# One rounding step of seven weight blocks per layer moved from GpSimd to ScalarE, in a two-layer hybrid backbone

## The reference

```python
def _token_mixers(h, pl, lambda_init, rope, ctx_kv):
    z = h @ pl['w_in']                  # 1024 -> 2816 columns: hyena 768, conformer 512, q, k, v 512 each
    ...
    if ctx_kv is None:
        k_all, v_all = k, v             # prompt: no rotation
    else:
        q = _apply_axial_rope(q, rope)  # sample: x*cos + partner(x)*sin
        k = _apply_axial_rope(k, rope)
        k_all = jnp.concatenate([ctx_kv[0].astype(dt), k], axis=1)
        v_all = jnp.concatenate([ctx_kv[1].astype(dt), v], axis=1)
    y_at = _diff_attention(q, k_all, v_all, lam, lambda_init, pl['subln_g'])
```

## Time and profile before

| | |
|---|---|
| time, median of 3 runs | 4292.77 us (4286.78 to 4298.58) |
| profiled execution, its own time | 4303.47 us |
| its span in the trace | 4301.5 us |
| mean granted TensorE clock | 0.943 of full |
| PE busy | 3737.7 us (87%) |
| DVE busy | 2407.0 us (56%) |
| POOL busy | 1510.2 us (35%) |
| ACT busy | 1052.5 us (24%) |

### The profile page before, as it was taken

The page is one execution under the profiler, slowest core; times in us unless marked ns, Lnnn a source line. Parts: engine busy times, 40 slices in busy tenths (PEclk is TensorE's granted clock), DMA queues, the critical chain, the costliest instruction groups (busy, mean ns, idle before and its releaser), DMA issues. The chain is left out here.

```text
span 4301.5 us, 51163 instructions
## 1 busy us (share of the span) xinstructions
PE 3737.7 (87%) x19550; PEld 3174.2 (74%) x19550; DVE 2407.0 (56%) x2998; ACT 1052.5 (24%) x1932; POOL 1510.2 (35%) x735
## 2 busy tenths in 40 slices
PE   7969989788759999999939998978794999999992
PEld 5768867577648888888828886767673888888881
DVE  2323554777575555555580365577667555555567
ACT  1011121367232111111141111147614111111115
POOL 0032656510242333323263275750033333223324
PEclk9999999899879999999968998989997999999996
DMA  5456654541301111111006664544220111111101
GB/s 155 129 185 194 184 167 121 169 112 59 113 20 30 40 40 35 37 38 40 20 16 204 198 178 155 160 137 100 77 89 10 40 40 37 33 40 40 40 11 49
DMA packets 360972, 380.86 MB, mean 89 GB/s; under 512 B 17951, under 2 KB 301709, under 8 KB 359470
## 3 DMA queue, kind: packets, MB, share of 16 engines
q1 hardware_dynamic: 247074, 233.40, 18.8%
q10 hardware_dynamic: 113676, 144.23, 10.4%
HBM read 286.34 MB, written 82.84 MB: 86 GB/s over the span
## 5 line engine op out<-in xcount | busy, mean ns | idle before, releaser
L638 POOL TENSOR_TENSOR RH<-RAW,ONE 128x1024 fp32r<-128x1024 f32 x256 | 504.1, 1969 | 2084.3 <-PE PS L730 863.8
L730 PE MATMUL PS<-HH,RH 128*128 128x512 f32 (+1 forms) x2784 | 615.1, 364 | 224.8 <-DVE HL L1683 63.8
L730 PEld LDWEIGHTS PS<-HH,RH 128*128 128x128 f32 x2784 | 479.3, 194 | 310.2 <-issue 154.7
L730 PE MATMUL PS<-HL,RH 128*128 128x512 f32 (+1 forms) x2784 | 701.7, 372 | 0.0
L640 POOL TENSOR_TENSOR RL<-RAW,RH 128x1024 fp32r<-128x1024 f32 x256 | 637.0, 2488 | 20.1
L730 PE MATMUL PS<-HH,RL 128*128 128x512 f32 (+1 forms) x2784 | 599.8, 358 | 0.0
L1919 DVE TENSOR_TENSOR SB<-RB 128x512 f32<-128x512 f32 (+1 forms) x192 | 205.5, 1070 | 644.0 <-ACT RB L1557 644.0
L1935 DVE SCALAR_TENSOR_TENSOR XT<-PS,ADA,XT 128x512 f32<-128x512 f32 (+1 forms) x768 | 474.2, 655 | 134.5 <-PE PS L1108 132.6
L730 PEld LDWEIGHTS PS<-HL,RH 128*128 128x128 f32 x2784 | 477.6, 193 | 57.3
L730 PEld LDWEIGHTS PS<-HH,RL 128*128 128x128 f32 x2784 | 466.3, 190 | 69.8
L1557 ACT ACTIVATE RB<-PS 128x512 f32<-128x512 f32 (+1 forms) x192 | 101.2, 527 | 1481.4 <-PE PS L730 1480.2
(11 more groups left out here) (224 smaller groups left out, 5370.9 us busy)
## 6 DMA issues: line engine op xcount, KB each, us to landing
RAW<-in_w_mlp_dram SPq DMA_DIRECT2D x128, 512.0 KB, 4.0
RAW<-const_dram SPq DMA_DIRECT2D x68, 512.0 KB, 3.9
ADW<-in_w_ada_dram ACTq DMA_DIRECT2D x60, 512.0 KB, 4.3
RAW<-in_w_in_dram SPq DMA_DIRECT2D x44, 512.0 KB, 4.7
ADW<-in_w_ada_dram SPq DMA_DIRECT2D x36, 512.0 KB, 3.7
x_scratch<-XT SPq DMA_DIRECT2D x4, 2560.0 KB, 13.8
z_scratch<-ZST ACTq DMA_DIRECT2D x40, 256.0 KB, 2.3
QH<-q_hi SPq DMA_DIRECT2D x32, 320.0 KB, 9.5
```

Source lines behind the costliest of these rows:

```text
L638: nc.gpsimd.tensor_tensor(RH[:, s, :], RAW[:, p, :], ONE[:].broadcast_to([128, 1024]), ALU.mult).then_inc(hi_split.sem, 1)
L730: mm = pe.matmul(out, w[:, s, k * 128:(k + 1) * 128], m(k), start=(n == 0 and k == 0), stop=(n == 2 and k == KT - 1))
```

## The change

For the seven blocks 17 to 23 of each layer (keys' last tile, the four value blocks, the first two forward-DFT blocks) the high part is made by ScalarE with an ACTIVATE Copy instead of by GpSimd; GpSimd waits for it on a new semaphore and makes the low part as before. ScalarE does this at the end of tiles 11 to 17, between the eight partner DMAs and `store_high`. GpSimd's own semaphore now counts 121 splits per layer. An unused semaphore is removed.

```diff
+FIRST_HI, SCALAR_HI = 17, 7
...
-        hi_split = signal("hi_split", BLOCKS)
+        hi_split = signal("hi_split", BLOCKS - SCALAR_HI)
+        hi_scalar = signal("hi_scalar", SCALAR_HI)
...
-        inv_done = signal("inv_done", 0)
...
                 pool.wait_ge(blk_used.sem, blk_used.at(l, b - RING + 1) + i * per_i)
-                nc.gpsimd.tensor_tensor(RH[:, s, :], RAW[:, p, :], ONE[:].broadcast_to([128, 1024]), ALU.mult).then_inc(hi_split.sem, 1)
-                pool.wait_ge(hi_split.sem, hi_split.at(l, b + 1) + i * per_i)
+                if FIRST_HI <= b < FIRST_HI + SCALAR_HI:
+                    pool.wait_ge(hi_scalar.sem, hi_scalar.at(l, b + 1 - FIRST_HI))
+                else:
+                    nc.gpsimd.tensor_tensor(RH[:, s, :], RAW[:, p, :], ONE[:].broadcast_to([128, 1024]), ALU.mult)\
+                      .then_inc(hi_split.sem, 1)
+                    own = b if b < FIRST_HI else b - SCALAR_HI
+                    pool.wait_ge(hi_split.sem, hi_split.at(l, own + 1) + i * per_i)
                 nc.gpsimd.tensor_tensor(RL[:, s, :], RAW[:, p, :], RH[:, s, :].bitcast(F32), ALU.subtract)\
...
+                def high_of_block(b):
+                    s, p = slot(l, b), b % 2
+                    act.wait_ge(raw_in[p].sem, raw_in[p].at(l, 16 * (b // 2 + 1)))
+                    act.wait_ge(blk_used.sem, blk_used.at(l, b - RING + 1))
+                    S.activation(RH[:, s, :], RAW[:, p, :], ACT.Copy).then_inc(hi_scalar.sem, 1)
...
                     if i >= 0:
                         partners(i)
+                    if 0 <= n + RING - FIRST_HI < SCALAR_HI:
+                        high_of_block(n + RING)
                     if i > 0:
                         store_high(i - 1)
```

## The result

The changed kernel takes 4327.86 us (median of 7 runs, 4315.74 to 4339.25) against 4292.14 us before (7 runs): ratio 1.0084, interval 1.0063 to 1.0105, that is 27 to 45 us slower. Forecast were 4330 us and slower.

A forecast was written before the change was run, and what follows sets the result against it. From tile 11 on, a ring of ACT and POOL, not PE, was taken to set the pace. Turns of 36.8 us plus 2 x 0.5 for the clock made 37.8; on 4292.77 that is 4330.6, predicted 4330, range 4311 to 4349.

The forecast's parts named there:

- The ring: ACT and POOL wait on each other per tile: high part, evacuation, DMA issue, landing, rotation; about 17.8 us a turn.
- the row of 579.51: Layer 0's last key transpose, behind the first value tile; its wait was read as ending 3.48 us before 579.51.
- Removed work: POOL's RH instruction, 14 times, 27.9 us, lying ahead of waits for partner DMAs; gain: nothing.
- The price of a turn: Eighth issue to next rotation 6.51 us, formerly the landing; five turns per layer, 17.5 and 17.1 us more.
- One sign of being right: POOL's RL of blocks 17 to 22 idles 5 to 7 us ahead of it, released by ACT's RH.
- The turn from tile 14 to 15: ACT itself is last there, with conformer store, load and sigmoid; the Copy costs its own length, 1.1 us.
- S: Stage from ScalarE's evacuation of tile 11's chunk 2 to the key transpose behind the first value tile; 110.2, 110.7 us before.
- PE's waits: ADW some 2 to 3 us around tile 15, then 6 to 8 us ahead of each key transpose; not added.
- The third rival: PE at 1.2 GHz for longer stretches, key tiles too; up to 28 us, half taken, 4345; chance 0.13.
- The clock's term: Slower PE clock around each layer's last wait; between 0 and 3.5 us per layer, 0.5 taken.

The follow-up runs named there:

- evac_first: The kernel before, with ScalarE evacuating chunk 2 ahead of the rotated head's high part instead of behind it: 4279.72 us, ratio 0.9956.
- copy_ahead: The changed kernel with ScalarE's Copy ahead of the eight partner DMAs instead of behind them: 4303.37 us, ratio 1.0012.
- both_mended: The changed kernel with chunk 2 evacuated first and the Copy ahead of the partner DMAs: 4280.85 us, ratio 0.9962.
- three_blocks: The changed kernel with only blocks 17, 18 and 19 getting their high part from ScalarE: 4315.43 us, ratio 1.0045.
- wait_only: The kernel before plus a 64-column ScalarE Copy of constants, awaited by GpSimd ahead of the low part of blocks 17 to 23: 4319.56 us, ratio 1.0046.

## Why the prediction was right

1. **The ring bounds the stage.** Right: evac_first takes PE's evacuation out of it and the waits of 15.0 us go. Two readings on the way were off. In the query tiles of layer 0 the ring did not set the pace: its turns there (17.09, 17.28 and 17.15 us between evacuations) were shorter than PE's 17.47. It was 1.8 us late at tile 11 and was catching up. And the row of 579.51 says that a wait of 3.48 us ended then, not that a wait had ended 3.48 us earlier. Neither enters the sum.
2. **Removed work gains nothing.** Right: GpSimd's 27.5 us less shows nowhere; in copy_ahead and both_mended, which also save them, there is no gain against the same order with GpSimd's own high part.
3. **The price of a turn.** From the eighth issue to the next rotation 6.51 us were forecast; 569.72 + 5.01 = 574.73 to 581.36 is 6.63 (the Copy starts 0.11 us behind the last issue and RL 0.16 behind the Copy's end, in place of 0.05 and 0.08). The five turns grew by 17.2 us in layer 0 and 16.7 in layer 1 (forecast 17.5 and 17.1). One sign of being right was misjudged: RL was to stand 5 to 7 us and stands 7.9, up to 10.6 at tiles 14 and 15, for between two rotations lie not only issue and Copy but the high part and the evacuation as well, 1.6 us; the sum counted these in the turn.
4. **The turn from tile 14 to 15 was mis-sized.** Forecast + 1.1 us for the Copy's length; measured 23.62 to 22.15 in layer 0 and 24.51 to 23.04 in layer 1, - 1.5 each. The Copy's length is no term there: the issue behind it starts 0.02 us after the Copy's start (574.84, 574.86), and in layer 0 it is 6.08 us from the evacuation to the issue of the conformer data's store, before and after. What fell is the gap from the end of that store's issue to the next load's, which waits for the store to land: 4.3 to 3.0 us in layer 0 and 5.5 to 3.0 in layer 1, where the partner issue took 1.0 us longer. This gap was 3.0 to 5.2 us in the other eight kernels, and 4.3 and 4.5 in three_blocks, whose tile 14 has no Copy; what moves it was not tried. This term is 5.1 of the 5.8 us by which the two stages grew less than forecast, 31.0 and not 36.8.
5. **The rest.** The median grew by 35.7 us, 4.7 more than the stages. The interval (27 to 45) holds both 31.0 and 36.8, so nothing is to be read from the difference, and that the median came within 3 us of 4330 is in part luck: by the stage the forecast was 5.8 us too high. In wait_only and three_blocks stage and median agree within 0.7 us. The two profiled executions differ by only 22.8 us in span; outside S the later one is 5.1 us shorter ahead of layer 0's key tiles, 6.9 shorter between the layers and 3.8 longer behind. Among the ten kernels the stretch between the layers varies from 1881.7 to 1892.0 us, so a single profile can't tell such a part from chance.
6. **PE's waits.** ADW: 2.40 us in layer 0, within the 2 to 3 forecast, and 0.47 in layer 1. At the last three transposes of a layer: 6.04, 4.49 and 4.04 us, and 5.37, 4.10 and 4.61, in place of 6 to 8; the first transpose, which had not waited, now waits 1.48 and 1.97. The waits are shorter because PE itself was slower in between, which is point 7. The last transpose came at 590.23 and not at about 598, as this execution reached the stage 5.1 us earlier and the stage grew by 15.8.
7. **The clock.** The third rival's mechanism was there, its price was not. Granted clock over the key tiles, first the kernel before, then the kernel after (columns as in the earlier trace rows):

```profile
540.00:597.00 57.00, 49.11 (x233) 40.53 (x232) 53.03 (x56) 12.29 (x19) 41.21 (x18) 0.97 0.49 147
```

```profile
540.00:608.00 68.00, 53.43 (x231) 43.72 (x230) 58.68 (x67) 14.06 (x21) 40.99 (x18) 0.87 0.47 140
```

With 0.87 over 68 us, the clock stood at 1.2 GHz for 2 x 0.13 x 68 = 17.7 us, against 3.4 before, part of it while PE waited. What it cost PE is read from PE's rows: behind the waits of 6.04 and 4.49 us PE worked 16.86 and 16.44 us up to its next wait (569.75 - 4.49 - 548.40 and 590.23 - 4.04 - 569.75), before it was 14.27 and 14.26. That is 4.8 us in layer 0, and in the same way 3.7 in layer 1, all of it inside turns of 20.5 us in which PE would have waited. The last wait of a layer is not covered. In layer 0 the granted clock about it is the same as before,

```profile
586.00:608.00 22.00, 17.96 (x73) 14.57 (x73) 19.28 (x37) 4.07 (x6) 13.78 (x7) 0.92 0.46 137
```

and from the transpose to the second value tile PE takes 7.36 us, 7.37 before. In layer 1 it takes longer. First before, then after:

```profile
2598.83 0.69 PE L841 MATMUL PS<-IDENT,ZRAW 128*128 128x128 f32 x2 [3.04 <-ACT ZRAW L1337]
...
2605.87 1.98 PE L854 MATMUL PS<-RH,HH 128*128 128x512 f32 x8
```

```profile
2617.86 0.69 PE L848 MATMUL PS<-IDENT,ZRAW 128*128 128x128 f32 x2 [4.61 <-ACT ZRAW L1351]
...
2625.76 1.98 PE L861 MATMUL PS<-RH,HH 128*128 128x512 f32 x8
```

That is 7.90 in place of 7.04 us (granted clock 0.84 from 2613 to 2635 us, 0.92 from 2594 to 2616 before). The clock's term, 2 x 0.5 us, came out as 0.0 + 0.9 in these two executions.
8. **Against the rule of the Trainium skill** (Perfetto Trace Analysis, Optimizing GPSIMD Operations): it says to prefer other engines to GpSimd where possible. The instruction did get shorter, 1.06 against 1.90 us, and the kernel longer. The rule is about the engine that does the work; here only the time of the handover counted, as copy_ahead and wait_only show.

## What to carry to other kernels

Before work is moved to an idle engine, read its queue, not its busy share: what stands ahead of the new instruction (DMA issues above all, 0.6 us each here) and what stands behind the wait on the engine that hands the work over. Where two engines hand a tile back and forth, draw one turn of that ring with its durations; only what lengthens or shortens the turn changes the time, and an evacuation that TensorE needs is best taken ahead of the ring's wait. Work that runs beside the ring can be cut down without any gain.

## What the runs showed of the hardware

- A DMA issue stands in ScalarE's queue ahead of the next ACTIVATE for its full time (eight partner DMAs 5.0 us, in some turns up to 6.2, four 2.45), while a running ACTIVATE does not hold up the issue behind it: it starts 0.02 to 0.13 us after the ACTIVATE.
- A semaphore from ScalarE to GpSimd costs little: from the Copy's end to the low part's start 575.90 to 576.06, 0.16 us.
- A slower TensorE clock, behind waits of 4 to 6 us, was hidden where TensorE was not the last to arrive (4.8 and 3.7 us of its time), and cost 0.9 us behind layer 1's last wait, where nothing covered it.
